# Logits of the windowed attention as two fp32r passes over stacked query parts, in a two-block network on one Trainium2 core

## What is computed

```python
def banded_window_attention(q, k, v, k_ctx, v_ctx, sink):     # 4 blocks of 128 latent queries
    ...
    def one_block(args):
        qn, kn, vn, valid_n = args
        s_win = jnp.einsum('bqhgd,bkhd->bhgqk', qn, kn).astype(jnp.float32) * scale
        s_win = jnp.where(valid_n, s_win, -jnp.inf)
        s_ctx = jnp.einsum('bqhgd,bchd->bhgqc', qn, k_ctx).astype(jnp.float32) * scale
        p = jax.nn.softmax(jnp.concatenate([s_win, s_ctx, s_sink], axis=-1), axis=-1)
        o = (jnp.einsum('bhgqk,bkhd->bqhgd', p[..., :nw], vn)
             + jnp.einsum('bhgqc,bchd->bqhgd', p[..., nw:nw + n_ctx], v_ctx))
...
def ab_mixer(...):
    ha_c, st_f, st_b = mlstm_bidir(*a_c, zero, zero)           # 2 chunks of 128, both directions
    ha_l, _, _ = mlstm_bidir(*a_l, st_f, st_b)                 # 4 chunks of 128, both directions
    ob_l = banded_window_attention(qb_l, kb_l, vb_l, kb_c, vb_c, sink)
    ob_c = gqa_attend(qb_c, kb_c, vb_c, sink)
```

## Time and profile before

| | before |
|---|---|
| median of 3 executions | 3305.35 us (3304.45 to 3305.71) |
| the profiled execution | 3304.75 us, its span 3303.0 us |
| TensorE busy in the span | 94%, mean granted clock 0.969 |
| VectorE, ScalarE, GpSimdE busy | 49%, 37%, 5% |
| recurrence, 1774 to 1858 us | TensorE 77.45 us busy, VectorE 56.42, ScalarE 35.31 |
| windowed attention, about 1861 to 1976 us | 48 units |

### The profile page before, as it was taken

One profiled execution on the slowest core, in us unless ns is written; L12 is line 12 of the kernel. 1 busy time (PEld: TensorE's weight loads), 2 busy tenths in 40 slices (PEclk: granted clock), 3 DMA queues, 4 the chain that ended last, 5 costly groups with the idle time before them and its releaser, 6 DMA issues. The chain is left out here.

```text
span 3303.0 us, 39562 instructions
## 1 busy us (share of the span) xinstructions
PE 3107.6 (94%) x15192; PEld 2483.6 (75%) x15192; DVE 1632.8 (49%) x2422; ACT 1238.2 (37%) x2046; POOL 155.1 (5%) x142
## 2 busy tenths in 40 slices
PE   6989999999998999998998998999999898899999
PEld 5666677776776677776885777788888775778887
DVE  4763666665454566674415543433333615344344
ACT  2543233335563233336114442423222424543332
POOL 2200000011000000000002001000000100000000
PEclk9969999999999999999998999999999999999999
DMA  5101443433201434431201001112121120022221
GB/s 189 52 25 40 178 157 136 177 106 52 77 1 58 175 124 178 152 109 39 64 26 52 1 1 52 51 51 76 51 76 51 51 77 0 1 77 102 102 87 65
DMA packets 157679, 259.17 MB, mean 78 GB/s; under 512 B 54332, under 2 KB 70074, under 8 KB 157436
## 3 DMA queue, kind: packets, MB, share of 16 engines
q1 hardware_dynamic: 155812, 252.66, 21.8%
q10 hardware_dynamic: 1628, 4.76, 0.4%
q0 software_dynamic: 128, 0.26, 0.0%
HBM read 255.57 MB, written 2.10 MB: 78 GB/s over the span
## 5 line engine op out<-in xcount | busy, mean ns | idle before, releaser
L1250 ACT ACTIVATE w_hi<-wbuf 128x1024 fp32r<-128x1024 f32 (+1 forms) x349 | 368.1, 1057 | 1227.4 <-PE psA L777 1163.9
L775 PE MATMUL psA<-act_hi,w_hi 128*128 128x512 f32 (+1 forms) x1872 | 707.5, 378 | 62.4 <-DVE act_lo L1929 37.1
L1923 DVE TENSOR_TENSOR w_lo<-wbuf,w_hi 128x1024 fp32r<-128x1024 f32 (+1 forms) x349 | 429.3, 1233 | 556.2 <-ACT w_hi L1250 551.0
L776 PE MATMUL psA<-act_lo,w_hi 128*128 128x512 f32 (+1 forms) x1872 | 701.4, 375 | 0.0
L777 PE MATMUL psA<-act_hi,w_lo 128*128 128x512 f32 (+1 forms) x1872 | 700.5, 374 | 0.0
L775 PE MATMUL psA<-hid_hi,w_hi 128*128 128x512 f32 (+1 forms) x1280 | 476.8, 373 | 5.4 <-DVE work L2032 4.5
L776 PE MATMUL psA<-hid_lo,w_hi 128*128 128x512 f32 (+1 forms) x1280 | 472.1, 369 | 0.0
L777 PE MATMUL psA<-hid_hi,w_lo 128*128 128x512 f32 (+1 forms) x1280 | 471.4, 368 | 0.0
L775 PEld LDWEIGHTS psA<-act_hi,w_hi 128*128 128x128 f32 x1872 | 358.8, 192 | 134.7 <-issue 52.1
L777 PEld LDWEIGHTS psA<-act_hi,w_lo 128*128 128x128 f32 x1872 | 357.7, 191 | 62.7
L776 PEld LDWEIGHTS psA<-act_lo,w_hi 128*128 128x128 f32 x1872 | 359.0, 192 | 60.9 <-issue 0.2
(11 more groups left out here) (271 smaller groups left out, 3562.8 us busy)
## 6 DMA issues: line engine op xcount, KB each, us to landing
wbuf<-in_mlp_w_dram SPq DMA_DIRECT2D x64, 2048.0 KB, 8.2
work<-in_ada_w_dram SPq DMA_DIRECT2D x32, 1536.0 KB, 10.9
wbuf<-in_ab_w_in_dram SPq DMA_DIRECT2D x10, 1024.0 KB, 5.0
wbuf<-in_ple_w_gate_dram SPq DMA_DIRECT2D x4, 2048.0 KB, 7.6
wbuf<-in_hy_w_in_dram SPq DMA_DIRECT2D x3, 2048.0 KB, 13.6
wbuf<-in_c_w_in_dram SPq DMA_DIRECT2D x3, 2048.0 KB, 7.6
wbuf<-in_hy_w_out_dram SPq DMA_DIRECT2D x2, 2048.0 KB, 7.8
wbuf<-in_mla_w_out_dram SPq DMA_DIRECT2D x2, 2048.0 KB, 8.3
```

Source lines behind the costliest of these rows:

```text
L775: pe.matmul(psA[:, s, a:b], w_hi, x_hi[:, a:b], start=first, stop=False)
L776: pe.matmul(psA[:, s, a:b], w_hi, x_lo[:, a:b], start=False, stop=False)
L1250: return nc.scalar.activation(out, in_, func, **kw)
L1923: tt(split_target(wL, stage, u), unit(v, stage, u, g), split_target(wH, stage, u), ALU.subtract).then_inc(S["w_split"], 1)
```

## The change

The logits of the windowed attention are made of fp32r operands. A query tile q is split into a rounded part (`hi`) and the rest (`lo`), and so are the keys. Stack tiles hold for each pair of heads the hi part of the even head in partitions 0 to 63 and its rest in 64 to 127 (`sw_even`), and the other way round for the odd head (`sw_odd`). The rounded keys (`sw_k_lat`, `sw_k_ctx`) lie in all 128 partitions, since the key rows are there twice. The first matmul of a part takes the stack (128 rows) with the rounded keys and so gives hi·hi + lo·hi; the second takes the 64 rows of the stack with hi and the rest of the keys (`sw_k_lo`).

```diff
+        SW_AT = WBUF_AT + 4 * KD * CW * ((first_chunk["ab_out"] + 1) % NW)
+        sw_even = split("sw_even", [P, 4, TOK], KD * TOK)
+        sw_odd = nc.alloc_sbuf_tensor_at("sw_odd", [P, 4, TOK], F32R, offset=SW_AT)
+        ... (sw_k_lat, sw_k_ctx, sw_k_lo, sw_turn: further fp32r tiles)
         def swa_logits(qt, h, lat=True):
-            r = slice(64 * (h % 2), 64 * (h % 2) + 64)
-            kv = 4 + h // (B_H // B_KV)
-            q = qkb[r, h // 2, (0 if lat else LAT) + qt * P:(0 if lat else LAT) + qt * P + P]
+            kv = h // (B_H // B_KV)
+            stack, r = ((sw_even, LOW), (sw_odd, HIGH))[h % 2]
+            cols = slice((0 if lat else LAT) + qt * P, (0 if lat else LAT) + qt * P + P)
+
+            def both(hi, lo):
+                return [(stack[:, h // 2, cols], hi), (stack[r, h // 2, cols], sw_k_lo[r, kv, lo])]
@@ SyncE
+                    if n == first_chunk["ab_out"] + 1:
+                        sp.wait_ge(t_ready[1], 6 * B_H // 2)
@@ ScalarE, in step u of the recurrence, behind the exponentials of u (decay_set), ahead of hs_square(u - 2)
+                if u < B_KV:
+                    f(sw_k_lat[:, u, :], qkb[:, 4 + u, 0:LAT], ACT.Copy)
+                    f(sw_k_ctx[:, u, :], qkb[:, 4 + u, LAT:TOK], ACT.Copy).then_inc(S["sw_hi"], 1)
+                elif u % 2 == 0 and u <= B_KV + B_H:
+                    c = (u - B_KV) // 2
+                    if c > 0:
+                        act.wait_ge(S["sw_lo"], c)
+                        f(sw_even[LOW, c - 1, :], qkb[LOW, c - 1, :], ACT.Copy)
+                    if c < 4:
+                        f(sw_odd[HIGH, c, :], qkb[HIGH, c, :], ACT.Copy)
+                        f(sw_turn[LOW, :], qkb[LOW, c, :], ACT.Copy).then_inc(S["sw_hi"], 1)
@@ VectorE, in step u of the recurrence, behind lstm_finish(u)
+                if 1 <= u <= B_KV:
+                    kv = u - 1
+                    v.wait_ge(S["sw_hi"], kv + 1)
+                    tt(sw_k_lo[:, kv, 0:LAT], qkb[:, 4 + kv, 0:LAT], sw_k_lat[:, kv, :], ALU.subtract)
+                    tt(sw_k_lo[:, kv, LAT:TOK], qkb[:, 4 + kv, LAT:TOK], sw_k_ctx[:, kv, :], ALU.subtract)
+                elif u % 2 == 1 and B_KV < u < B_KV + B_H:
+                    c = (u - B_KV) // 2
+                    v.wait_ge(S["sw_hi"], B_KV + c + 1)
+                    tt(sw_odd[LOW, c, :], qkb[HIGH, c, :], sw_odd[HIGH, c, :], ALU.subtract)
+                    v.drain()
+                    tt(sw_even[HIGH, c, :], qkb[LOW, c, :], sw_turn[LOW, :], ALU.subtract).then_inc(S["sw_lo"], 1)
```

More of the change, by code:

```diff
@@ L126, in build @@
         xT = sb("xT", [P, KD, TOK])
+        PT_AT = -(-nc.sbuf_base // 32) * 32
         pT = sb("pT", [P, 2, 2, LAT])
@@ L271, in build @@
         S = {n: sem(n) for n in (
-            "centered", "squared", "sum_ready", "sum_read", "mean_read", "acc_set", "acc_mean", "ple_set", "tile_sum", "norm_set", "acc_zero", "relu_used", "gate_used", "act_hi", "act_split", "w_hi", "w_split", "g_hi", "hidden_set",
+            "centered", "squared", "sum_ready", "sum_read", "mean_read", "acc_set", "acc_mean", "ple_set", "tile_sum", "sw_hi", "sw_lo", "norm_set", "acc_zero", "relu_used", "gate_used", "act_hi", "act_split", "w_hi", "w_split", "g_hi", "hidden_set",
             "ada_used", "ada_sum", "row_ready", "row_set", "row_turned", "conv_set", "vec_set", "sqrt_set", "lam_exp", "lam_set",
@@ L512, in window @@
             return list(range(max(qt - 1, 0), min(qt + 2, LT)))
-        def swa_logits(qt, h, lat=True):
-            r = slice(64 * (h % 2), 64 * (h % 2) + 64)
-            kv = 4 + h // (B_H // B_KV)
-            q = qkb[r, h // 2, (0 if lat else LAT) + qt * P:(0 if lat else LAT) + qt * P + P]
+        SW_AT = WBUF_AT + 4 * KD * CW * ((first_chunk["ab_out"] + 1) % NW)
+        sw_even = split("sw_even", [P, 4, TOK], KD * TOK)
+        sw_odd = nc.alloc_sbuf_tensor_at("sw_odd", [P, 4, TOK], F32R, offset=SW_AT)
+        sw_k_lat = nc.alloc_sbuf_tensor_at("sw_k_lat", [P, B_KV, LAT], F32R, offset=SW_AT + 16 * TOK)
+        sw_k_ctx = split("sw_k_ctx", [P, B_KV, CTX], late + 2 * TOK + 9 * P)
+        sw_k_lo = split("sw_k_lo", [P, B_KV, TOK], KD * TOK + 4 * TOK)
+        sw_turn = nc.alloc_sbuf_tensor_at("sw_turn", [P, TOK], F32R, offset=PT_AT + 4 * 2 * STATE)
+        LOW, HIGH = slice(0, 64), slice(64, 128)
+        def swa_logits(qt, h, lat=True):
+            kv = h // (B_H // B_KV)
[3 more added lines that the diff above has]
+                return [(stack[:, h // 2, cols], hi), (stack[r, h // 2, cols], sw_k_lo[r, kv, lo])]
             at, parts = 0, []
@@ L521, in swa_logits @@
                 at = len(w) * P
-                parts.append((0, at, [(q, qkb[r, kv, w[0] * P:w[0] * P + at])]))
+                keys = slice(w[0] * P, w[0] * P + at)
+                parts.append((0, at, both(sw_k_lat[:, kv, keys], keys)))
             for a, b in ((0, P), (P, CTX)) if at + CTX > 512 else ((0, CTX),):
-                parts.append((at + a, at + b, [(q, qkb[r, kv, LAT + a:LAT + b])]))
+                parts.append((at + a, at + b, both(sw_k_ctx[:, kv, a:b], slice(LAT + a, LAT + b))))
             return parts
```

## The result

| | before | changed |
|---|---|---|
| median of the executions | 3305.53 us | 3351.1 us (3344.09, 3347.28, 3354.91 and 6196.25) |
| ratio to before, 95% interval | | 1.0128 (1.0108 to 1.0148) |
| the profiled execution | 3304.75 us | 3354.91 us, span 3353.1 |
| recurrence, first filler to first logits | 86.86 us | 121.09 us |
| attention, first logits to the output projection's first matmul | 135.50 us | 151.23 us |

A forecast was written before the change was run, and what follows sets the result against it. TensorE, busy 94% of the span, was taken as the bound, with VectorE only .26 us a step behind in the recurrence. Recurrence +24.3 and attention -4.1 made +20.2 on 3305.35: 3325 us, range 3309 to 3336.

The forecast's parts named there:

- VectorE's additions: Recurrence: ten new subtractions on VectorE's chain cost 10.0 us, less 2.1 for its used-up idle time.
- ScalarE's wait: Recurrence: ScalarE waits for the second subtraction, so its copies, squares and exponentials delay VectorE's weighing and mask: +11.9 us.
- The clock in the recurrence: Recurrence: stalls idle TensorE and lower its clock, so values run slower: +4.5 us, bounds 0 and 8.
- The attention: Windowed attention: fewer column costs, -16.6 us, against changes of the row count, +12.5: -4.1, bounds -16.6 and +5.4.
- The old change ahead of the logits: Windowed attention: row-count change before a unit's logits; each kind's two old changes .03 us cheaper each, .06 off per kind.
- kind C: Windowed attention's context-block units: .56 us forecast from first logits to transposes, where before it was .63.
- What hides: ScalarE's first copies fit its idle time, else 1 us a step; output projection's weights arrive in time, else up to 5.
- (a): Rival, attention: the change of rows costs nothing, +7.7 us in all, 3313 us; chance .12.
- (b): Rival, attention: fp32r matmuls of 128 columns cost what f32 ones do, +29.7 us in all, 3335 us; chance .12.
- (c): Rival, recurrence: ScalarE doesn't bind, so stalls and clock loss fall away, +3.8 us in all, 3309 us; chance .08.
- (d): Rival, recurrence: the subtractions are hidden on VectorE, so the kernel gets no slower; at nothing added, 3301 us; chance .03.

The follow-up runs named there:

- experiment 1: The changed kernel with ScalarE's copies for query pairs 1 to 3 and the last copy one step later: 3326.26 us, ratio 1.0058.
- experiments 2 and 3: Each against the changed kernel: first, second pass over all 128 rows, 3319.17 us; then, every second part does its 64-row matmul first, 3334.81 us.

## Why the prediction was wrong

The direction and the places were right, and the size was not: 20 us forecast, 42 measured by the ratio and 50 in the profiled execution. Two terms failed, the clock behind the stalls and the attention. Term by term, for the profiled execution:

- **VectorE's additions, 10.0 - 2.1 = +7.9.** Right: 6.8 with the circle undone.
- **ScalarE's wait, +11.9.** Right: 13.0 by the distances of experiment 1. The mask stands 6.58 us behind the subtractions of step 3, where 5.25 + 1.17 = 6.42 was the working, and 2.55 without, for 2.60.
- **The clock in the recurrence, +4.5, bounds 0 to 8: 12.1 measured.** I took "1.2 us for each of three stalls", the values at half clock, because the rows of before show half clock only at the end, where values are all that is left. Behind a stall in the middle, the filler and the scores of the step after next stand ahead of the values in TensorE's queue: 5.87 + 3.44 us at .50 for 3.04 + 1.79, 4.5 us more behind the first stall, and 3.2 and 4.0 behind the next two. The filler in the idle times brought 10.9 of it back. My upper bound of 8 was too low for the same reason.
- **The attention, -4.1, bounds -16.6 and +5.4: +6.5 at the full clock.** That changes of rows eat up what the columns save was right, and the sizes were off. A change costs .19 (256 columns follow in .31 instead of .12) rather than .16: from logits to transposes the three kinds take 1.23, 1.75 and .61 us, where I had 1.12, 1.57 and .56, 16 x .34 = 5.4 more. The old change ahead of the logits, which I took off at .18 a unit, gave back .12, .13 and .05: 3.8. And the first two units had been done side by side before (below): 1.4. -4.1 + 10.6 = +6.5.
- **The clock in kind C and behind it, not in the sum: +9.2.** I had read in the earlier trace rows that TensorE goes without a wait, and gave the stage no clock. The fall comes at the end of 8 us in which it idled .38. It needn't have come: the other two executions, 3344.09 and 3347.28, are near 3354.91 - 11.2 = 3343.7; whether they ran at the full clock there was not seen.
- **The start of the recurrence, not in the sum: +2.3**, which other kernels with the same instructions didn't have.
- **What hides** hid: ahead of the output projection TensorE waits 7.53 us for the split weights, before 7.54.

The clock in kind C and the late start were not in every kernel with these instructions. Without them the profiled execution would still be some 39 us over the kernel before, above my 3336. So the prediction failed at two steps of its own: the clock behind the stalls, 7.6 us too low because only the values were counted, and the price of the changes of rows in the attention, 10.6 us too low with what goes with it.

The rivals: (a) and (b) fell by experiments 2 and 3, (c) by the 3.71 us of idle, (d) by the 6.8 us of experiment 1. By the rule of the Trainium skill that I had weighed ("TensorE: Matmul & The Clock Gate", "Step-by-step: what each phase is for", the row count doesn't matter for a load's time) the attention would have been -16.6. What the rule says of a load this trace agrees with: one of 64 rows takes .18 us in the changed kernel and one of 128 rows .19. What does not follow from it is that changes are free. The logits with changes of rows took +6.5 and those without -18.2, so what costs is the change between neighbours, of which this rule says nothing.

## What to carry over

A wait on an engine's list is priced by what stands behind it, and a stall that empties TensorE is priced again by all work that the next step has in TensorE's queue, at half clock: nearly twice the step up to the keys (9.3 us for 4.8), not only the matmul that was waited for. Copies that prepare something for later go behind a point that their releaser has long passed; one step later gave back 25 us of the recurrence's 34. Where operands may have full height (here with a rest that was in all partitions anyway), matmuls with fewer rows between others with 128 are not cheaper, each change costs .17 to .19 us, and one edit of a slice took 25 us from the changed attention and made it 18 us shorter than before, up to its last logits. The clock made stretches with the same instructions differ by 2 us and more from one profiled kernel to the next, so a difference of that size is read only beside the granted clock of its parts.

## What the hardware showed beyond that

Before the change, the first two units of the attention, an even and an odd head whose 64 rows are different halves of the array, were done side by side. Timeline of TensorE in the kernel before, then in the changed kernel:

```profile
1860.88 1.14 PE L901 MATMUL psA<-work 64*128 64x256 f32 x8
1861.96 3.70 PE L731 MATMUL psO<-const 128*128 128x512 f32 x8
```

```profile
1896.54 0.39 PE L918 MATMUL psA<-sw_k_lat,sw_even 128*128 128x256 f32 x1
...
1899.04 3.70 PE L748 MATMUL psO<-const 128*128 128x512 f32 x8
```

Four f32 matmuls of 256 columns take 1.08 us there, where two of one head take 1.06; with the stacks the same two units take 2.50. An order that put even and odd heads next to each other throughout was not tried.
